# A decoder trunk on one core: the order of two weight rests, the key rests and the maxima in VectorE's stream of the attention heads

## The chip, the core and the metric

The kernel runs on one core of one Trainium2 chip. A core has TensorE for matrix products (the profile splits it into PE, the matmuls, and PEld, the loads of their stationary operand), VectorE (DVE), ScalarE (ACT), GpSimd (POOL) and SyncE (SP), which issues the transfers. Each engine works through its own list of instructions in order, and engines wait for one another by semaphores. The metric is the device time of one execution in microseconds, the median of three runs.

## The reference

Input `x` has 512 tokens of 1024 features in float32. Two layers, each:

```python
h = h + 0.5 * _swiglu(_rmsnorm(h, ffn1_norm[l]), ffn1_w1[l], ffn1_w3[l], ffn1_w2[l])
u = _rmsnorm(h, mix_norm[l])
z = u @ w_in[l]          # q, k, v of three attention branches, forget logits, gates
o_a = _diff_attention(...)         # 4 heads, difference of two softmaxes
o_b = _forgetting_attention(...)   # 8 heads, softmax with a forget bias
o_c = _stick_breaking_attention(...)   # 8 heads
m = sum of gates[:, :, i] * (o_i @ proj_i[l]);  h = h + m @ w_out[l]
h = h + 0.5 * _swiglu(_rmsnorm(h, ffn2_norm[l]), ...)
```

The branch that matters here is the second one:

```python
logits = (jnp.einsum('bqhd,bkhd->bhqk', qb, k).astype(f32) * scale
          + cq[..., :, None] - c[..., None, :])
logits = jnp.where(dist >= 0, logits, -jnp.inf)
p = jax.nn.softmax(logits, axis=-1)
return jnp.einsum('bhqk,bkhe->bhqe', p.astype(v.dtype), v)
```

## The kernel before

**Products in parts.** Every float32 operand of a product is split into a rounded part (`hi`, made by ScalarE) and a rest (`lo`, made by VectorE as operand minus rounded part), and `three` (L724) multiplies hi by hi, hi by lo and lo by hi. A *weight rest* is therefore one VectorE instruction over a whole unit of weights: `split(k)` (L2034) waits for ScalarE's rounded part and writes `w_lo` of slot `k`, 128 x 1024 elements. Its semaphore `w_set` lets TensorE use the slot and lets SyncE load the next unit into the raw slot (`load_next`, L600).

**The heads.** The attention runs over four tiles of 128 columns (two heads of the branches with 64-wide heads) in each of two layers, so the code in question runs 8 times: in the chain of waits its transposes start at 413.79, 484.89, 556.01 and 627.10 us (tiles 0 to 3 of the first layer) and at 1619.90, 1690.99, 1762.11 and 1833.22 us (the second layer). Within one tile every engine has its list written out by hand: `heads` of TensorE at L1105, of ScalarE at L1732, of VectorE at L2699. TensorE fills its time between attention steps with `unit(...)`: 8 blocks of three 512-column matmuls each, which project queries or keys for later steps.

**The piece around the change.** TensorE's list has this order (each step named by its line in the profile): `turn_probs(0)` (L1003, transposes of the third branch's weights), a unit up to block 6 (L726 to L728), `weighted(t, 2, 1)` (L1047), `scores(1, 0)` (L981, the second branch's first head), the rest of the unit, `unit(own[3], 2, 0, 4)` (12 matmuls with slot 2), `turn_probs(0)` again (L1003, ten transposes of the probabilities of `scores(1, 0)`), and the remaining blocks. Three waits matter:

- `scores(1, 0)` waits on `qk_set` for two steps of VectorE, the last of which is `qk_lo(1, 2, 1)`: the *rests of the second branch's keys*, two instructions of 64 x 512. That step in turn waits on `qk_hi_set` for ScalarE's `qk_hi(1, 2, 1)` (four ACTIVATEs of 64 x 512).
- `turn_probs` waits on `prob_set` once for each block `i` of 128 queries, ahead of the block's `i + 1` transposes (1, 2, 3 and 4). VectorE makes each block in two steps: `block_max` (L2576), a masked copy of the scores with their maximum, and `share_out` (L2582), a reciprocal (L2585) and a scaling (L2588), the *quotients*. Between them ScalarE takes the exponential, `exps` (L1655, in the profile L1659), one for each block.
- `unit(own[3], 2, ...)` waits on `w_set` for the rest of slot 2, and the next tile's `unit(0, 0)` for the rest of slot 0, `split(0)`.

`output_whole(1)` (L2666, in the profile L2669) adds the two parts of an attention output and waits for ScalarE's `output_rest(1)`. `turned_lo` (L2613, in the profile L2032 `area<-ps,area`) makes the rests of transposed probabilities. Nearly all rests show line L2032, so in the profile they are told apart by their tiles: `w_lo<-w_raw,w_hi` is a weight rest, `area<-scratch_whole,area` 64 x 512 a query or key rest.

Of the kernel before, what the change touches and what calls it, by code (L numbers as in the profile page):

```python
# [192 lines left out]
def trunk(nc, x, stream, params, const, const_r, const_b, out):  # L193
    ctx = ExitStack()
    with ctx:
# [57 lines left out]
        def half(hd):  # L253

            return slice(hd * HEAD, (hd + 1) * HEAD)
# [9 lines left out]
        def q_twice(branch, hd):  # L265
            return qk_tile(branch % 2 * 8 + hd)

        def k_both(branch, hd):
            return qk_tile(branch % 2 * 8 + 2 + hd)
# [3 lines left out]
        def q_rest(branch, hd):  # L273
            return qk_tile(16 + hd if branch == 2 else branch * 8 + 4 + hd)
# [26 lines left out]
        def tile(k):  # L301
            return scratch[:, k * SEQ:(k + 1) * SEQ]
# [963 lines left out]
        def neg_max(buf, i):  # L1266
            return stat[:, 4 * buf + i:4 * buf + i + 1]

        def total(buf, i):
            return stat[:, 8 + 4 * buf + i:9 + 4 * buf + i]  # L1270

        def inverse(buf, i):
            return stat[:, 16 + 4 * buf + i:17 + 4 * buf + i]
# [17 lines left out]
        def keys(part, j):  # L1291

            return area[:, part + PT_OFF[j]:part + PT_OFF[j] + (NQ - j) * P]

        def query_block(buf, i):
            return prob[buf][:, Q_OFF[i]:Q_OFF[i] + (i + 1) * P]
# [726 lines left out]
        def _(dve):  # L2023
# [7 lines left out]
            def lo(dst, src, hi_part):  # L2031
                return dve.tensor_tensor(dst, src, hi_part.bitcast(F32), ALU.subtract)  # L2032

            def split(k, raw=None, blocks=UNIT):  # L2034
                dve.wait_ge(w_hi_set, c.next(w_hi_set))
                at = slice(k * UNIT * P, (k * UNIT + blocks) * P)
                raw = k if raw is None else raw
                lo(w_lo[:, at], w_raw[:, raw * UNIT * P:(raw * UNIT + blocks) * P], w_hi[:, at]).then_inc(w_set, 1)
                c.skip(w_set)
# [520 lines left out]
            def qk_lo(branch, which, k):  # L2560
                dve.wait_ge(qk_hi_set, c.next(qk_hi_set))
                for hd in range(2):
                    src = tile(k)[half(hd), :]
                    if which == 0:
                        last = lo(q_rest(branch, hd)[half(hd), :], src, q_twice(branch, hd)[half(hd), :])
                    else:
                        last = lo(k_both(branch, hd)[half(1 - hd), :], src, k_both(branch, hd)[half(hd), :])
                last.then_inc(qk_set, 1)
                c.skip(qk_set)
# [6 lines left out]
            def block_max(buf, i):  # L2576
                dve.wait_ge(score_set, scored.next())
                dve.tensor_tensor_reduce(query_block(buf, i), ps[:, SB0 + i, 0:(i + 1) * P],  # L2578
                                         causal_w[:, (NQ - 1 - i) * P:], -1.0, FAR, ALU.add, ALU.min,
                                         neg_max(buf, i)).then_inc(max_set, 1)  # L2580

            def share_out(buf, i, done):  # L2582

                dve.wait_ge(exp_set, c.next(exp_set))
                dve.reciprocal(inverse(buf, i), total(buf, i)).then_inc(vec_done, 1)  # L2585
                dve.wait_ge(vec_done, c.next(vec_done))
                q = query_block(buf, i)
                dve.tensor_scalar(q, q, inverse(buf, i), None, ALU.mult).then_inc(done, 1)  # L2588
                c.skip(done)
# [23 lines left out]
            def turned_lo(j):  # L2613
                dve.wait_ge(pt_hi_set, c.next(pt_hi_set))
                lo(keys(PT_LO, j), ps[:, SB0 + j, 0:(NQ - j) * P], keys(PT_HI, j)).then_inc(pt_set, 1)
# [19 lines left out]
            def output_square_lo():  # L2635

                dve.wait_ge(o_sq_hi_set, c.next(o_sq_hi_set))
                lo(o_sq_lo, tile(7), o_sq_hi).then_inc(o_sq, 1)
# [37 lines left out]
            def rest_of_tile(t, layer, next_unit):  # L2676

                turned_lo(0)
                turned_lo(1)
                turned_lo(2)  # L2680
                turned_lo(3)
                next_unit(0, 0, SCALE)
                values_split() if t < NT else split(0)
                block_max(0, 0)
                block_max(0, 1)
                block_max(0, 2)
                block_max(0, 3)
                output_whole(1)
                share_out_all(0)
                block_max(1, 0)  # L2690
                block_max(1, 1)
                block_max(1, 2)
                block_max(1, 3)
                next_unit(1, 1, 1.0)
                split(1)
                output_lo(1, t - 1)
                differences(layer)

            def heads(t, layer, before):  # L2699

                if before:
                    rest_of_tile(t, layer, take)
                    qk_lo(2, 0, 0)
                    qk_lo(2, 2, 1)
                    turned_lo(0)
                    turned_lo(1)
                    turned_lo(2)
                    turned_lo(3)
                    values_lo(t, 0, before)
                    values_lo(t, 1, before)  # L2710
                    output_square_lo()
                c.skip(unit_done, 3)
                stick_runs(0)
                stick_runs(1)
                stick_weights(0)
                stick_runs(2)
                stick_weights(1)
                stick_runs(3)
                stick_weights(2)
                stick_weights(3)  # L2720
                if not before:
                    values_lo(t, 0, before)
                    values_lo(t, 1, before)
                    sums_of_forget(layer)
                split(2)
                if before:
                    output_normed(layer)
                    output_lo(0, t - 1)
                turned_lo(0)
                turned_lo(1)  # L2730
                turned_lo(2)
                turned_lo(3)
                values_lo(t, 2, before)
                values_lo(t, 3, before)
                split(0)
                split(1)
                output_whole(0)
                stick_runs(0)
                stick_runs(1)
                stick_weights(0)  # L2740
                stick_runs(2)
                stick_weights(1)
                stick_runs(3)
                stick_weights(2)
                stick_weights(3)
                banks = (AUX, 0, 1, AUX) if before else (0, AUX, 1, AUX)
                take(0, banks[0], SCALE)
                rows(t * 2, 1, 0)
                rows(t * 2 + 1, 1, 1)
                rows(t + N_FOX, 0, 0)  # L2750
                rows(t + N_FOX, 0, 1)
                take(1, banks[1], 1.0)
                qk_lo(1, 0, 0)
                turned_lo(0)
                turned_lo(1)
                turned_lo(2)
                turned_lo(3)
                split(2)
                qk_lo(1, 2, 1)
                split(0)  # L2760
                output_whole(1)
                block_max(0, 0)
                block_max(0, 1)
                block_max(0, 2)
                block_max(0, 3)
                share_out(0, 0, prob_set)
                share_out(0, 1, prob_set)
                share_out(0, 2, prob_set)
                share_out(0, 3, prob_set)
                take(0, banks[2], SCALE)  # L2770
                split(1)
                turned_lo(0)
                turned_lo(1)
                turned_lo(2)
                turned_lo(3)
                take(1, banks[3], 1.0)
                block_max(1, 0)
                block_max(1, 1)
                block_max(1, 2)
                block_max(1, 3)  # L2780
                qk_lo(0, 0, 0)
                share_out(1, 0, prob_set)
                output_lo(2, t)
                share_out(1, 1, prob_set)
                share_out(1, 2, prob_set)
                share_out(1, 3, prob_set)
                output_whole(0)
                qk_lo(0, 2, 1)
                split(2)
# [152 lines left out]
            def mixer(layer, gain):  # L2942
                forget(layer)
                heads(0, layer, False)
                for t in range(1, NT):
                    heads(t, layer, True)
# [254 lines left out]
```

## Time and profile before

| what | value |
|---|---|
| median of 3 runs | 2435.03 us (2434.97 to 2435.12) |
| profiled execution | 2435.02 us |
| its span, first to last instruction | 2433.0 us |
| PE busy / PEld busy | 2421.7 us (100%) / 2226.9 us (92%) |
| DVE busy / ACT busy | 2125.6 us (87%) / 1498.7 us (62%) |
| granted TensorE clock | 1.000 over the span |
| one tile of the heads, from 484.89 to 556.01 | 71.12 us |

The profiled execution lasted 2.02 us more than its span, and it lies 0.01 us from the median. PE's busy time counts pipelined matmuls whose ends are modelled, so a busy share of 100% does not say that no matmul waited: a wait shows in the distance between the starts of two neighbours, and in the idle time ahead of a weight load.

### The profile page before, as it was taken

To read this page: it belongs to the slowest core of one execution; us is meant where nothing else is said; L and a number is where in the kernel's file an instruction comes from. 1 tells how busy PE (TensorE), PEld (TensorE's weight loads), DVE (VectorE), ACT (ScalarE), POOL (GpSimd) and SP (SyncE) were. 2 spreads that over 40 slices of the span, in tenths; PEclk is the share of its full clock that TensorE was granted. 3 is DMA by queue.
4 is the path that set the end of the run, shared out by engine and by line. 5 is a ranking of instruction groups with operands and counts; after the bars stand their busy time and mean duration, and the time that the engine had idled before them with its cause. 6 is when DMAs were issued, how large, how long until landed. Compare 5 with 4: busy or idle time off the path is not lost.

```text
span 2433.0 us, 48313 instructions
## 1 busy us (share of the span) xinstructions
PE 2421.7 (100%) x15618; PEld 2226.9 (92%) x15618; DVE 2125.6 (87%) x3968; ACT 1498.7 (62%) x2951; POOL 3.2 (0%) x10
## 2 busy tenths in 40 slices
PE   9999999999999999999999999999999999999999
PEld 8999888888899889998889998888888998899988
DVE  8999878989898779998799997799988986899986
ACT  6666457788754456664366664578786554566643
POOL 0000000000000000000000000000000000000000
PEclk9999999999999999999999999999999999999999
DMA  4333322222232323333333323322212333233332
GB/s 166 110 103 104 113 96 69 70 62 69 71 113 80 112 87 105 104 106 117 109 94 109 103 95 105 111 72 61 70 61 70 104 109 101 87 109 104 115 113 78
DMA packets 64676, 233.72 MB, mean 96 GB/s; under 512 B 7168, under 2 KB 7552, under 8 KB 64512
## 3 DMA queue, kind: packets, MB, share of 16 engines
q1 hardware_dynamic: 64368, 231.58, 29.4%
q8 instruction: 85, 1.39, 0.2%
q14 instruction: 79, 0.65, 0.1%
q10 hardware_dynamic: 144, 0.10, 0.0%
HBM read 229.55 MB, written 2.10 MB: 95 GB/s over the span
## 4 chain that ended last, share of the span: by engine, by line
PE 87%; DVE 6%; ACT 4%; issue 3%; DMA 0%; DVEq 0%; ACTq 0%; SPq 0%
PE ps L726 26%; PE ps L728 26%; PE ps L727 26%; DVE area L2032 2%; PE ps L1047 2%; PE ps L981 1%; ACT area L1311 1%; PE ps L1029 1%; PE ps L1031 1%; PE ps L1030 1%; ACT scratch_whole L1659 1%; PE ps L1003 1%; DVE w_lo L2032 1%; DVE scratch_whole L2578 1%; DVE scratch_whole L2598 0%
## 5 line engine op out<-in xcount | busy, mean ns | idle before, releaser
L1311 ACT ACTIVATE w_hi<-w_raw 128x512 fp32r<-128x512 f32 (+2 forms) x882 | 623.0, 717 | 481.4 <-PE ps L728 218.7
L2032 DVE TENSOR_TENSOR w_lo<-w_raw,w_hi 128x512 fp32r<-128x512 f32 (+2 forms) x882 | 699.2, 800 | 102.2 <-ACT w_hi L1311 84.8
L726 PE MATMUL ps<-u_hi,w_hi 128*128 128x256 f32 (+1 forms) x2240 | 708.5, 316 | 0.0
L728 PE MATMUL ps<-u_hi,w_lo 128*128 128x256 f32 (+1 forms) x2240 | 706.0, 315 | 0.0
L727 PE MATMUL ps<-u_lo,w_hi 128*128 128x256 f32 (+1 forms) x2240 | 705.6, 315 | 0.0
L727 PE MATMUL ps<-area,w_hi 128*128 128x256 f32 (+1 forms) x1778 | 583.3, 328 | 0.0
L726 PE MATMUL ps<-area,w_hi 128*128 128x512 f32 (+1 forms) x1414 | 482.3, 341 | 1.0 <-ACT scratch_whole L1417 0.9
L728 PE MATMUL ps<-area,w_lo 128*128 128x512 f32 (+1 forms) x1414 | 480.1, 340 | 0.0
L728 PEld LDWEIGHTS ps<-u_hi,w_lo 128*128 128x128 f32 x2240 | 427.1, 191 | 27.2
L726 PEld LDWEIGHTS ps<-u_hi,w_hi 128*128 128x128 f32 x2240 | 427.2, 191 | 26.7 <-DVE w_lo L2032 0.5
L727 PEld LDWEIGHTS ps<-u_lo,w_hi 128*128 128x128 f32 x2240 | 427.3, 191 | 25.9
L727 PEld LDWEIGHTS ps<-area,w_hi 128*128 128x128 f32 x1778 | 338.1, 190 | 29.2
L726 PEld LDWEIGHTS ps<-area,w_hi 128*128 128x128 f32 x1414 | 268.1, 190 | 32.5 <-DVE w_lo L2032 1.6
L728 PEld LDWEIGHTS ps<-area,w_lo 128*128 128x128 f32 x1414 | 268.1, 190 | 29.5
L726 PE MATMUL ps<-v_area,w_hi 128*128 128x256 f32 x880 | 249.4, 283 | 0.0
L728 PE MATMUL ps<-v_area,w_lo 128*128 128x256 f32 x880 | 249.0, 283 | 0.0
L1417 ACT ACTIVATE scratch_whole<-ps 128x256 f32<-128x256 f32 x376 | 141.7, 378 | 151.9 <-PE ps L728 150.2
L726 PEld LDWEIGHTS ps<-v_area,w_hi 128*128 128x128 f32 x880 | 168.9, 192 | 0.4 <-DVE w_lo L2032 0.2
L728 PEld LDWEIGHTS ps<-v_area,w_lo 128*128 128x128 f32 x880 | 168.9, 192 | 0.0
L1311 ACT ACTIVATE area<-scratch_whole 64x512 fp32r<-64x512 f32 (+1 forms) x202 | 123.6, 627 | 38.7 <-DVE scratch_whole L2558 14.2
L727 PE MATMUL ps<-v_area,w_hi 128*128 128x256 f32 x440 | 124.5, 283 | 0.0
L2032 DVE TENSOR_TENSOR area<-scratch_whole,area 64x512 fp32r<-64x512 f32 (+1 forms) x120 | 82.3, 686 | 12.5 <-ACT area L1311 11.2
(214 smaller groups left out, 3172.6 us busy)
## 6 DMA issues: line engine op xcount, KB each, us to landing
w_raw<-weights SPq DMA_DIRECT2D x432, 512.0 KB, 3.7
h<-x SPq DMA_DIRECT2D x4, 512.0 KB, 6.5
out<-scratch_whole SPq DMA_DIRECT2D x8, 256.0 KB, 2.4
scratch_whole<-const_b SPq DMA_DIRECT2D x1, 512.0 KB, 9.5
scratch_whole<-const_r SPq DMA_DIRECT2D x1, 192.0 KB, 8.7
cst<-const SPq DMA_DIRECT2D x1, 137.0 KB, 8.1
par<-params ACTq DMA_DIRECT2D x1, 98.0 KB, 4.5
```

Of the source, the lines that this page charges most:

```text
L726: pe.matmul(dst, hi, x_hi, start=start, stop=False, **kw)
L727: pe.matmul(dst, hi, x_lo, start=False, stop=False, **kw)
L728: return pe.matmul(dst, lo, x_hi, start=False, stop=stop, **kw)
L981: last = pe.matmul(ps[:, SB0 + i, 0:n], queries[part][:, i * P:n], keys_of[part][:, 0:n], start=part == 0, stop=part == 1)
L1003: last = pe.transpose(ps[:, SB0 + j, (i - j) * P:(i - j + 1) * P], prob[buf][:, at:at + P], ident)
L1029: pe.matmul(dst, x_hi, w_hi[:, of], start=k == 0, stop=False)
L1030: pe.matmul(dst, x_lo, w_hi[:, of], start=False, stop=False)
L1031: last = pe.matmul(dst, x_hi, w_lo[:, of], start=False, stop=k == UNIT - 1)
L1047: last = pe.matmul(ps[:, OB, SEQ - n:SEQ], v, area[:, at + PT_OFF[j]:at + PT_OFF[j] + n], start=(j, part) == (0, 0), stop=(j, part) == ste ...
L1311: return act.activation(dst, src, ACT.Copy)
L1417: act.activation(to, half_bank((of or banks(s))[2 if n == 1 else 0]), ACT.Copy).then_inc(snap_set, 1)
L2032: return dve.tensor_tensor(dst, src, hi_part.bitcast(F32), ALU.subtract)
```

## The change

In VectorE's list of `heads` the rests of the second branch's keys, `qk_lo(1, 2, 1)`, stand ahead of the rest of slot 2 and no longer behind it. The rest of slot 0 stands behind the four maxima and ahead of the four quotients, and no longer ahead of `output_whole(1)` and the maxima. No instruction is added or removed, and the lists of the other engines are the same.

```diff
--- before.py
+++ after.py
@@ -2755,14 +2755,14 @@
                 turned_lo(1)
                 turned_lo(2)
                 turned_lo(3)
+                qk_lo(1, 2, 1)
                 split(2)
-                qk_lo(1, 2, 1)
-                split(0)
                 output_whole(1)
                 block_max(0, 0)
                 block_max(0, 1)
                 block_max(0, 2)
                 block_max(0, 3)
+                split(0)
                 share_out(0, 0, prob_set)
                 share_out(0, 1, prob_set)
                 share_out(0, 2, prob_set)
```

The first place is VectorE's list in tile 1 of the first layer, from the last instruction of `turned_lo` on; `64x512 x2` is the pair of key rests, `w_lo` is slot 2 first and slot 0 second. Before:

```order
L2032 TENSOR_TENSOR area<-ps,area 128x128
L2035 REGISTER_ALU
L2032 TENSOR_TENSOR w_lo<-w_raw,w_hi 128x1024
L2561 REGISTER_ALU
L2032 TENSOR_TENSOR area<-scratch_whole,area 64x512 x2
L2035 REGISTER_ALU
L2032 TENSOR_TENSOR w_lo<-w_raw,w_hi 128x1024
L2668 REGISTER_ALU
L2669 TENSOR_TENSOR w_raw<-ps,w_raw 64x512
L2578 ISA scratch_whole,stat<-ps,masks 128x128
```

Now:

```order
L2032 TENSOR_TENSOR area<-ps,area 128x128
L2561 REGISTER_ALU
L2032 TENSOR_TENSOR area<-scratch_whole,area 64x512 x2
L2035 REGISTER_ALU
L2032 TENSOR_TENSOR w_lo<-w_raw,w_hi 128x1024
L2668 REGISTER_ALU
L2669 TENSOR_TENSOR w_raw<-ps,w_raw 64x512
L2578 ISA scratch_whole,stat<-ps,masks 128x128
```

The key rests have moved up past the first weight rest, and the second weight rest is gone from ahead of L2669.

The second place is a few instructions further on, from the last of the four maxima (L2578, of the block of 512 keys) to the first two quotients. Before:

```order
L2578 ISA scratch_whole,stat<-ps,masks 128x512
L2578 ISA stat 128x1
L2584 REGISTER_ALU
L2585 RECIPROCAL stat<-stat 128x1
L2586 REGISTER_ALU
L2588 TENSOR_SCALAR scratch_whole<-scratch_whole,stat 128x128
L2584 REGISTER_ALU
L2585 RECIPROCAL stat<-stat 128x1
L2586 REGISTER_ALU
L2588 TENSOR_SCALAR scratch_whole<-scratch_whole,stat 128x256
```

Now:

```order
L2578 ISA scratch_whole,stat<-ps,masks 128x512
L2578 ISA stat 128x1
L2035 REGISTER_ALU
L2032 TENSOR_TENSOR w_lo<-w_raw,w_hi 128x1024
L2584 REGISTER_ALU
L2585 RECIPROCAL stat<-stat 128x1
L2586 REGISTER_ALU
L2588 TENSOR_SCALAR scratch_whole<-scratch_whole,stat 128x128
L2584 REGISTER_ALU
L2585 RECIPROCAL stat<-stat 128x1
L2586 REGISTER_ALU
L2588 TENSOR_SCALAR scratch_whole<-scratch_whole,stat 128x256
```

The rest of slot 0 stands between the last maximum and the first reciprocal. The same two places differ in all 8 tiles.

## Rows read from the trace of the kernel before

**Rows 1.** Busy time by engine of one stretch: PE, PEld, DVE, ACT, POOL, PEclk, DMA

```profile
469.31:484.89 15.58, 15.58 (x80) 13.16 (x79) 14.77 (x35) 12.41 (x25) 0.00 (x0) 1.00 0.21 68
```

**Rows 2.** Timeline of VectorE, tile 1: start us, us, line, what [idle before <- releaser]

```profile
476.55 1.21 DVE L2032 TENSOR_TENSOR w_lo<-w_raw,w_hi 128x1024 fp32r<-128x1024 f32 x1
477.79 1.39 DVE L2032 TENSOR_TENSOR area<-scratch_whole,area 64x512 fp32r<-64x512 f32 x2
479.21 1.22 DVE L2032 TENSOR_TENSOR w_lo<-w_raw,w_hi 128x1024 fp32r<-128x1024 f32 x1
480.47 0.69 DVE L2669 TENSOR_TENSOR w_raw<-ps,w_raw 64x512 f32<-64x512 f32 x1
...
482.23 0.69 DVE L2578 CUSTOM_DVE_ANT_0 scratch_whole<-ps,masks 128x512 f32<-128x512 f32 x1
...
482.84 0.16 DVE L2585 RECIPROCAL stat<-stat 128x1 f32<-128x1 f32 x1
...
484.42 0.49 DVE L2588 TENSOR_SCALAR scratch_whole<-scratch_whole,stat 128x512 f32<-128x512 f32 x1
...
486.65 1.68 DVE L2032 TENSOR_TENSOR area<-ps,area 128x512 fp32r<-128x512 f32 x4
488.76 0.69 DVE L2558 SCALAR_TENSOR_TENSOR scratch_whole<-ps,rstd 128x512 f32<-128x512 f32 x1 [0.42 <-PE ps L728]
490.31 0.29 DVE L2578 CUSTOM_DVE_ANT_0 scratch_whole<-ps,masks 128x128 f32<-128x128 f32 x1 [0.86 <-PE ps L981]
```

**Rows 3.** Timeline of ScalarE, the same tile

```profile
475.36 2.31 ACT L1311 ACTIVATE area<-scratch_whole 64x512 fp32r<-64x512 f32 x4
...
483.82 0.19 ACT L1659 ACTIVATION_READ_ACCUMULATOR scratch_whole<-scratch_whole,stat 128x1 f32 x1
...
499.13 1.17 ACT L1311 ACTIVATE w_hi<-w_raw 128x128 fp32r<-128x128 f32 x2
```

**Rows 4.** Timeline of TensorE's matmuls, the same tile

```profile
479.23 1.54 PE L981 MATMUL ps<-area 128*128 128x128 f32 x8
...
484.49 0.40 PE L728 MATMUL ps<-u_hi,w_lo 128*128 128x512 f32 x1
484.73 1.26 PE L1003 MATMUL ps<-cst,scratch_whole 128*128 128x128 f32 x10
485.74 0.48 PE L726 MATMUL ps<-u_hi,w_hi 128*128 128x512 f32 x1
```

**Rows 5.** Timeline of TensorE's weight loads between 485.38 and 485.50

```profile
485.28 0.36 PEld L1003 LDWEIGHTS ps<-cst,scratch_whole 128*128 128x128 f32 x3
```

**Rows 6.** Timelines of four engines, tile 0

```profile
404.34 2.31 ACT L1311 ACTIVATE area<-scratch_whole 64x512 fp32r<-64x512 f32 x4
...
406.69 1.39 DVE L2032 TENSOR_TENSOR area<-scratch_whole,area 64x512 fp32r<-64x512 f32 x2 [0.18 <-ACT area L1311]
...
413.31 0.49 DVE L2588 TENSOR_SCALAR scratch_whole<-scratch_whole,stat 128x512 f32<-128x512 f32 x1
...
413.39 1.25 PEld L1003 LDWEIGHTS ps<-cst,scratch_whole 128*128 128x128 f32 x10
...
414.63 0.48 PE L726 MATMUL ps<-u_hi,w_hi 128*128 128x512 f32 x1
```

**Rows 7.** Timelines, other transposes behind VectorE (the last tile's differences)

```profile
653.55 1.94 DVE L2610 SCALAR_TENSOR_TENSOR scratch_whole<-scratch_whole,stat 128x128 f32<-128x128 f32 x4
...
655.54 0.42 PEld L1003 LDWEIGHTS ps<-cst,scratch_whole 128*128 128x128 f32 x4 [0.35 <-DVE scratch_whole L2610]
...
654.38 1.81 PE L1003 MATMUL ps<-cst,scratch_whole 128*128 128x128 f32 x10
...
655.95 0.47 PE L726 MATMUL ps<-u_hi,w_hi 128*128 128x512 f32 x1
```

**Rows 8.** Waits of weight loads: waiter <- releaser: us, times, longest

```profile
PEld ps L1047 <- DVE area L2032: 7.7, 22, 0.5
```

**Rows 9.** The page, DMA issues: count, KB each, median us to landing

```profile
w_raw<-weights SPq DMA_DIRECT2D x432, 512.0 KB, 3.7
```

## The prediction, made before the changed kernel was run

> **What bounds the kernel now.** I read the busy times first. In the table of the profile PE is busy for the whole span and VectorE for 87% of it. In the 15.6 us ahead of the transposes in question PE is busy for all of it and VectorE for 14.77 us, at a granted clock of 1.00; the same stretch of the other seven tiles agrees within 0.4 us for PE and 0.1 us for VectorE [rows 1]. So TensorE sets the time, VectorE has next to no room beside it, and every moment for which VectorE makes TensorE wait is added to the end. Then I read the waits. TensorE hardly waits here: all rests of that kind hold its weight loads back for 7.7 us in 22 places over the span [rows 8]. What matters is therefore not what the removed waits cost, but which new one appears. For that I read the timelines of VectorE, ScalarE and TensorE side by side in tile 1, and ask at each step who is waited for.
>
> **Part one, the key rests ahead of the weight rest of slot 2.** Before, this weight rest runs from 476.55 to 477.76 and the key rests from 477.79 to 479.18 [rows 2]. They need ScalarE's rounded keys, and these end at 475.36 + 2.31 = 477.67 [rows 3]. So moved up, the key rests can't start with the weight rest's 476.55; VectorE waits until 477.67 and starts at about 477.70 (in tile 0 the same step starts 0.04 us after ScalarE's end: 404.34 + 2.31 = 406.65 against 406.69 [rows 6]). The gain is 477.79 - 477.70 = 0.09 us, and 1.1 us in which VectorE did a weight rest become idle. TensorE starts the scores at 479.23 [rows 4], 0.05 us behind the end of the key rests; it may start them up to 0.09 us earlier. In tile 0 the step already waits for ScalarE, so nothing is gained there. The rest of slot 2 now runs from about 479.1 to 480.35. Its user, the unit ahead of the transposes, has 12 matmuls; L1003 starts at 484.73, 0.24 us behind the last of them [rows 4], and 12 such distances put the unit's start near 481.9. It is covered by 1.5 us, so I cost it at nothing. Without that cover it would cost 1.2 us a tile.
>
> **Part two, the rest of slot 0 ahead of the quotients.** `output_whole` starts at 480.47 before. Now it follows the rest of slot 2, which holds the place that the rest of slot 0 had; it starts 0.09 us earlier, and so do the maxima. Before, the first reciprocal starts at 482.84, right behind the last maximum, whose main part started at 482.23 and lasted 0.69 us [rows 2]. Now a weight rest stands there. How much it puts between its own start and the next start the rows bound: 1.26 us (479.21 to 480.47) and 1.24 us (476.55 to 477.79) on the one side [rows 2]; on the other, its duration of 1.22 us less the 0.08 us by which the reciprocal starts before the maximum's end (482.92 - 482.84), so 1.14 us. I take 1.20. The quotients thus shift by 1.20 - 0.09 = 1.11 us in the six later tiles and by 1.20 in tile 0 of each layer.
>
> Does something hide that? ScalarE's last exponential ends at 483.82 + 0.19 = 484.01 [rows 3], and the first ones long before 482.84: before the change the quotients wait for VectorE's own queue, not for ScalarE, so the weight rest fills no gap there.
>
> What is late next are the transposes. The last quotient ends at 484.42 + 0.49 = 484.91 [rows 2], and the first of the four weight loads that need it starts at 485.28 [rows 5] (the seventh of ten). The margin is 0.37 us, against a shift of 1.11. The new end of the last quotient is 484.91 + 1.11 = 486.02. What TensorE does with a late block the trace shows elsewhere: the differences end at 653.55 + 1.94 = 655.49, the seventh weight load starts at 655.54, and the next unit's matmul at 655.95 [rows 7]: 0.05 us, then 0.41 us. By these the load starts at 486.07 and the unit at 486.48, against 485.74 before [rows 4]: 0.74 us. In tile 0 the last quotient ends at 413.31 + 0.49 = 413.80, now 415.00; the unit starts at 415.46 against 414.63 [rows 6]: 0.83 us.
>
> **Whether it passes on.** The next step of VectorE that takes its time from TensorE comes soon: it has idle times of 0.42 us (until 488.76, for a unit) and 0.86 us (until 490.31, for the scores of the other head) [rows 2]. VectorE reaches them 1.11 us later, TensorE 0.74 us later; the 0.37 us between are less than the first idle time. From 490.31 on the two stand to each other as before, all 0.74 us later. The probability rests between (486.65 before [rows 2], now near 487.8) are needed by a weighted product that starts at about 489.3 now, 12 matmuls of 0.24 us behind 486.48: covered. The raw slot 0 is released near 484.0 and not at 480.43; the next unit takes 3.7 us to land [rows 9] and ScalarE reads it at 499.13 [rows 3]: covered by over 11 us.
>
> Sum: 6 x 0.74 + 2 x 0.83 = 6.1 us, with 1.14 and 1.26 for the open distance 5.6 and 6.6. On the profiled execution's own 2435.02 us that is 2441.1 us; the median of the runs, 2435.03, is the same for this purpose.
>
> **A rule weighed.** In the stretch of [rows 1] the weight loads are busy for 13.16 of 15.58 us. The Trainium skill, Perfetto Trace Analysis, section Identifying the Most-Contended Engine, says that matmul busy time is no measure of TensorE's headroom and the weight loads' busy share is. By that rule TensorE would have 16% in hand here, and a stall of 0.74 us would be made up within 5 us: no change. The trace doesn't show such a recovery: behind the late transposes of [rows 7] the ten take 655.95 - 654.38 = 1.57 us against 485.74 - 484.73 = 1.01 us undisturbed [rows 4]: 0.56 us longer, of which the 0.35 us that the seventh weight load waited is a part, and nothing came faster than in the undisturbed case.
>
> **The rivals.**
> 1. *The stall is made up* (2435.0 to 2437.3 us, within 0.2%). For it: TensorE waits later in a tile anyway, 7.7 us over the 22 places [rows 8], 0.96 us a tile. If those waits ended at fixed times the new stall would take their place and all of it would vanish (2435.0); if half of them did, 6.1 - 8 x 0.48 = 2.3 us are left (2437.3). Against it: the rests that end them hang on maxima that start when TensorE's scores arrive (idle 0.86 us for L981 [rows 2]), so they shift as well.
> 2. *The quotients keep up, and only the earlier keys count* (2434.5 us, not slower). Place: the last quotient of each tile. If the weight rest came out of VectorE's way, the last quotient would end before 485.23 in tile 1 (0.05 us ahead of the load at 485.28), and the scores up to 0.09 us earlier in six tiles would be all: -0.5 us. It decides where the shift is below 0.32 us. For it stands only that VectorE overlaps neighbours by some hundredths; against it 1.22 us of work against a margin of 0.37.
> 3. *A second stall behind the first* (2444.7 us). The probability rests start 1.11 us later and the weighted product then waits: if the product needed all four rests at its start, 487.8 + 1.68 = 489.45 against 489.3, and the same happened again at the next head, 0.45 us a tile would come on top: 6.1 + 3.6 = 9.7 us. Against it: the product takes the rests one after another, and the last of them only behind several matmuls.
>
> **How the numbers follow.** What a measurement of this kernel can tell from no change is about 0.2%, 4.9 us. The forecast has 76%, rival 1 has 11%, rival 2 has 4%, rival 3 has 5%, and 4% is left for a smaller stall. The forecast's own range is 2440.6 to 2441.7, all of it slower by over 0.2% (from 2439.9 on), though it would take only 0.15 us less in each tile to fall under that bound; I leave 4% of the forecast's case for it. Rival 2 lies within 0.2% too, and no case that I can name is faster by more; 2% stand for one that I can't. So slower 0.77, same 0.21, faster 0.02. The range for 8 times in 10 is 2438.0 to 2442.5.
>
> **What would show it.** In the changed profile VectorE should be idle for about 1.1 us ahead of the key rests, for ScalarE. L1003's weight loads should wait for L2588 in all 8 tiles, 6 to 7 us in all (no such row exists before), its ten transposes should take about 1.75 us from start to the next unit, and the tile should last 71.8 to 71.9 us. It is wrong if the ten take 1.01 us as before; if they take longer but the tile lasts 71.1 us, rival 1 holds; if the weighted product (L1047) behind them gains a wait, rival 3.

## The result and the profile after

The changed kernel takes 2441.01 us (median of 12 runs, 2440.52 to 2441.26) against 2435.27 us of the kernel before beside it (12 runs, 2434.97 to 2435.82): 1.0023 times as long, 95% interval 1.0015 to 1.0031. 2441.1 us were forecast: 6.1 us more than the 2435.03 of before, where 5.74 us were measured (2441.01 - 2435.27). The profiled execution took 2440.52 us with a span of 2438.6 us, 5.6 us more than the span before, at a granted clock of 1.00.

VectorE in tile 1 of the changed kernel (start us, us, line, what, idle before and its releaser), to be laid beside [rows 2]:

```profile
478.48 1.39 DVE L2032 TENSOR_TENSOR area<-scratch_whole,area 64x512 fp32r<-64x512 f32 x2 [1.06 <-ACT area L1311]
479.90 1.23 DVE L2032 TENSOR_TENSOR w_lo<-w_raw,w_hi 128x1024 fp32r<-128x1024 f32 x1
481.15 0.69 DVE L2669 TENSOR_TENSOR w_raw<-ps,w_raw 64x512 f32<-64x512 f32 x1
...
482.92 0.69 DVE L2578 CUSTOM_DVE_ANT_0 scratch_whole<-ps,masks 128x512 f32<-128x512 f32 x1
...
483.53 1.22 DVE L2032 TENSOR_TENSOR w_lo<-w_raw,w_hi 128x1024 fp32r<-128x1024 f32 x1
484.67 0.16 DVE L2585 RECIPROCAL stat<-stat 128x1 f32<-128x1 f32 x1
...
486.24 0.49 DVE L2588 TENSOR_SCALAR scratch_whole<-scratch_whole,stat 128x512 f32<-128x512 f32 x1
...
488.37 1.68 DVE L2032 TENSOR_TENSOR area<-ps,area 128x512 fp32r<-128x512 f32 x4
490.23 0.69 DVE L2558 SCALAR_TENSOR_TENSOR scratch_whole<-ps,rstd 128x512 f32<-128x512 f32 x1 [0.18 <-PE ps L728]
491.78 0.29 DVE L2578 CUSTOM_DVE_ANT_0 scratch_whole<-ps,masks 128x128 f32<-128x128 f32 x1 [0.85 <-PE ps L981]
```

All of this tile lies 0.77 us later than before, by what tile 0 lost, so only distances within the tile can be compared. ScalarE's keys end here:

```profile
476.14 2.31 ACT L1311 ACTIVATE area<-scratch_whole 64x512 fp32r<-64x512 f32 x4
```

at 476.14 + 2.31 = 478.45, and VectorE, idle for 1.06 us, starts the key rests at 478.48. From the end of ScalarE's keys to the last maximum it is 482.92 - 478.45 = 4.47 us; before it was 482.23 - 477.67 = 4.56 [rows 2, 3]. So the move up gained the 0.09 us that ScalarE left to gain. From the last maximum to the last quotient it is 486.24 - 482.92 = 3.32 us against 484.42 - 482.23 = 2.19: 1.13 us more, which is the weight rest that stands there now.

TensorE's weight loads for the transposes at the same place:

```profile
485.20 0.14 PEld L1003 LDWEIGHTS ps<-cst,scratch_whole 128*128 128x128 f32 x1
485.66 0.20 PEld L1003 LDWEIGHTS ps<-cst,scratch_whole 128*128 128x128 f32 x2 [0.32 <-DVE scratch_whole L2588]
486.19 0.31 PEld L1003 LDWEIGHTS ps<-cst,scratch_whole 128*128 128x128 f32 x3 [0.33 <-DVE scratch_whole L2588]
486.78 0.42 PEld L1003 LDWEIGHTS ps<-cst,scratch_whole 128*128 128x128 f32 x4 [0.28 <-DVE scratch_whole L2588]
```

and its matmuls, the ten transposes and the first of the unit behind:

```profile
485.42 2.02 PE L1003 MATMUL ps<-cst,scratch_whole 128*128 128x128 f32 x10
487.19 0.48 PE L726 MATMUL ps<-u_hi,w_hi 128*128 128x512 f32 x1
```

Before, the ten loads were one row without idle time (in tile 0 they are shown in [rows 6]). Now each block of quotients behind the first is waited for, and the unit behind starts 487.19 - 485.42 = 1.77 us after the first transpose, not 1.01 [rows 4]. In tile 0 the unit starts at 415.40 instead of 414.63: 0.77 us. In tile 1 the transposes take 0.76 us longer, but TensorE reaches them 0.08 us earlier in the tile, since the scores ahead of them can start earlier; from tile 0's unit to tile 1's it is 487.19 - 415.40 = 71.79 us, against 485.74 - 414.63 = 71.11 before, a loss of 0.68 us. Over the span the waits of weight loads (us, times, longest) read

```profile
PEld ps L1047 <- DVE area L2032: 7.8, 22, 0.5
PEld ps L1003 <- DVE scratch_whole L2588: 7.4, 24, 0.3
```

L2588 is new, 24 times, which is three blocks in each of eight tiles; L1047 is what it was [rows 8]. The three waits of a tile add up to 0.93 us and the transposes take only 0.76 us longer. A part of such a wait costs nothing, because the loads run ahead of their matmuls: the first by 485.42 - 485.20 = 0.22 us.

### The profile page after: what moved, and what is told of

Same layout as the page of the kernel before. It is cut to its first block, busy times and chain, and to the rows that moved or that the text cites. A ratio compares the mean times of both kernels' runs of the same rounds, so it can differ in the third digit from the quotient of the medians.

```text
span 2438.6 us, 48313 instructions
## 1 busy us (share of the span) xinstructions
PE 2425.6 (99%) x15618; PEld 2225.2 (91%) x15618; DVE 2125.1 (87%) x3968; ACT 1498.4 (61%) x2951; POOL 3.2 (0%) x10
## 4 chain that ended last, share of the span: by engine, by line
PE 82%; DVE 9%; ACT 5%; issue 4%; DVEq 0%; DMA 0%; ACTq 0%; SPq 0%
PE ps L726 25%; PE ps L727 25%; PE ps L728 25%; ACT area L1311 3%; DVE area L2032 2%; DVE w_lo L2032 2%; PE ps L1047 1%; PE ps L1029 1%; PE ps L1031 1%; PE ps L1030 1%; ACT scratch_whole L1659 1%; DVE scratch_whole L2578 1%; PE ps L1003 1%; DVE scratch_whole L2623 1%; PE ps L981 1%
## 5 line engine op out<-in xcount | busy, mean ns | idle before, releaser
L726 PE MATMUL ps<-u_hi,w_hi 128*128 128x256 f32 (+1 forms) x2240 | 708.8, 316 | 0.5 <-DVE w_lo L2032 0.5
L726 PE MATMUL ps<-area,w_hi 128*128 128x512 f32 (+1 forms) x1414 | 482.3, 341 | 1.0 <-ACT scratch_whole L1417 0.9
L726 PEld LDWEIGHTS ps<-u_hi,w_hi 128*128 128x128 f32 x2240 | 427.2, 191 | 27.7 <-DVE w_lo L2032 1.7
L726 PEld LDWEIGHTS ps<-area,w_hi 128*128 128x128 f32 x1414 | 268.1, 190 | 32.8 <-DVE w_lo L2032 1.6
L726 PE MATMUL ps<-v_area,w_hi 128*128 128x256 f32 x880 | 249.4, 283 | 0.0
L1417 ACT ACTIVATE scratch_whole<-ps 128x256 f32<-128x256 f32 x376 | 141.5, 377 | 151.8 <-PE ps L728 150.1
L726 PEld LDWEIGHTS ps<-v_area,w_hi 128*128 128x128 f32 x880 | 168.9, 192 | 0.4 <-DVE w_lo L2032 0.2
```

The lines of the kernel that those rows point to most:

```text
L726: pe.matmul(dst, hi, x_hi, start=start, stop=False, **kw)
L1417: act.activation(to, half_bank((of or banks(s))[2 if n == 1 else 0]), ACT.Copy).then_inc(snap_set, 1)
```

## The experiments

The first question was which of the two moves costs, and whether a late quotient is paid in full. Each group of kernels ran on one chip together with the kernel before, and each time is compared with the time of the kernel before on that chip.

**Only the key rests moved.**

```diff
-                split(2)
                 qk_lo(1, 2, 1)
+                split(2)
                 split(0)
                 output_whole(1)
```

> Only the key rests are moved ahead of the rest of slot 2; the rest of slot 0 stays ahead of output_whole and the maxima. Theory (the key rests wait 1.1 us for ScalarE and everything behind them is late, wherever the second weight rest stands): output_whole starts 1.15 to 1.25 us later than before, the last quotient too, and the ten transposes of the branch's first head stall as in the changed kernel: +5.3 to +6 us, about 2441 us. Rival (what costs is the weight rest between the maxima and the quotients, and the earlier keys cost nothing): 2434.7 to 2435.4 us, no wait of L1003 for L2588.

Measured: 2440.88 us against 2435.24, ratio 1.0023 (1.0014 to 1.0032): all of the loss, with the rest of slot 0 still ahead of `output_whole`. VectorE's rows:

```profile
478.36 1.39 DVE L2032 TENSOR_TENSOR area<-scratch_whole,area 64x512 fp32r<-64x512 f32 x2 [1.06 <-ACT area L1311]
479.78 2.36 DVE L2032 TENSOR_TENSOR w_lo<-w_raw,w_hi 128x1024 fp32r<-128x1024 f32 x2
482.17 0.69 DVE L2669 TENSOR_TENSOR w_raw<-ps,w_raw 64x512 f32<-64x512 f32 x1
...
486.12 0.49 DVE L2588 TENSOR_SCALAR scratch_whole<-scratch_whole,stat 128x512 f32<-128x512 f32 x1
```

VectorE's idle 1.06 us reach `output_whole`: it starts 482.17 - 478.36 = 3.81 us behind the start of the key rests, where before it started 480.47 - 477.79 = 2.68 us behind it [rows 2], because now both weight rests stand between. That is 1.13 us more (1.15 to 1.25 were expected), while the key rests themselves gain at most 0.09. L1003 waits for L2588 for 7.4 us in 24 places, as in the changed kernel. The rival, by which the earlier keys cost nothing and only a weight rest ahead of the quotients costs, falls: the first move alone is enough.

**Only the rest of slot 0 moved.**

```diff
                 split(2)
                 qk_lo(1, 2, 1)
-                split(0)
                 output_whole(1)
                 block_max(0, 0)
                 block_max(0, 1)
                 block_max(0, 2)
                 block_max(0, 3)
+                split(0)
```

> Only the rest of slot 0 is moved behind the maxima; the key rests stay behind the rest of slot 2. Theory: output_whole, freed of 1.25 us of queue, can only start 0.5 us earlier in the later tiles because ScalarE's part ends at 479.94 in the trace before (0.9 us earlier in tile 0), then the weight rest adds 1.14 to 1.2: the last quotient is 0.65 to 0.7 us late in six tiles and 0.25 to 0.3 in two, against a margin of 0.37. So 6 x 0.3 = 1.8 to 2 us more, about 2437.2 us. Rival (the move costs the whole weight rest, 1.2 - 0.37 a tile, whatever stands in front): 2441.5 us.

Measured: 2436.88 us (2436.68 to 2437.39) against 2435.24 (2435.02 to 2435.74); the ratio's interval, 0.9998 to 1.0016, includes 1, but the two sets of runs don't overlap. VectorE's rows:

```profile
480.15 0.69 DVE L2669 TENSOR_TENSOR w_raw<-ps,w_raw 64x512 f32<-64x512 f32 x1 [0.80 <-ACT w_raw L1699]
...
485.23 0.49 DVE L2588 TENSOR_SCALAR scratch_whole<-scratch_whole,stat 128x512 f32<-128x512 f32 x1
```

and the last four weight loads of the transposes:

```profile
485.77 0.42 PEld L1003 LDWEIGHTS ps<-cst,scratch_whole 128*128 128x128 f32 x4 [0.28 <-DVE scratch_whole L2588]
```

Without the weight rest in front, VectorE comes to `output_whole` early and waits there for ScalarE, 0.80 us (0.35 us in tile 0). So of the 1.25 us that the move frees ahead of `output_whole` only a part is used, and the whole weight rest comes back ahead of the quotients. The last quotient is late by the difference, and only the last block is waited for: loads of L1003 wait 1.7 us for L2588 in 6 places, none of them in tile 0. That makes 1.6 us where 1.8 to 2 were expected; the rival's 2441.5 us falls.

**The rest of slot 0 behind the quotients**, with the key rests moved and without.

```diff
+                qk_lo(1, 2, 1)
                 split(2)
-                qk_lo(1, 2, 1)
-                split(0)
                 output_whole(1)
...
                 share_out(0, 3, prob_set)
+                split(0)
```

> The key rests are moved up as in the changed kernel, and the rest of slot 0 stands behind the quotients instead of ahead of them. Theory (the quotients alone carry the loss): no wait of L1003 for L2588; the probability rests behind come about 1.1 us later than before and just miss the weighted product by 0.1 to 0.15 us a tile, the scores start 0.08 us earlier: 2435.0 to 2436.2 us. Rival (VectorE is so full that the same 1.1 us of idling costs the same wherever it surfaces): 2440 to 2441 us, with new waits of L1047.

> The key rests stay behind the rest of slot 2, the rest of slot 0 stands behind the quotients. Theory: the quotients end 0.5 us earlier than before, which nobody uses, and the probability rests start about 0.75 us later, in time for the weighted product: within 0.5 us of before, 2435.3 us. Rival (as above, lost VectorE time costs wherever it surfaces): 0.75 - 0.37 us a tile or more, 2438 us.

Measured: 2434.95 us (2434.71 to 2435.3) with the key rests moved, 2435.35 (2435.03 to 2435.86) without (where `split(2)` and `qk_lo` keep their order), against 2435.24: ratios 0.9999 (0.9990 to 1.0008) and 1.0001 (0.9992 to 1.0010), which can't be told from no difference. In the first, VectorE idles as in the changed kernel, and the quotients are not late:

```profile
477.65 1.39 DVE L2032 TENSOR_TENSOR area<-scratch_whole,area 64x512 fp32r<-64x512 f32 x2 [1.06 <-ACT area L1311]
...
484.27 0.49 DVE L2588 TENSOR_SCALAR scratch_whole<-scratch_whole,stat 128x512 f32<-128x512 f32 x1
...
487.54 1.68 DVE L2032 TENSOR_TENSOR area<-ps,area 128x512 fp32r<-128x512 f32 x4
...
490.21 0.29 DVE L2578 CUSTOM_DVE_ANT_0 scratch_whole<-ps,masks 128x128 f32<-128x128 f32 x1 [0.39 <-PE ps L981]
```

and TensorE's transposes and unit:

```profile
484.58 1.26 PE L1003 MATMUL ps<-cst,scratch_whole 128*128 128x128 f32 x10
485.59 0.48 PE L726 MATMUL ps<-u_hi,w_hi 128*128 128x512 f32 x1
```

The unit starts 1.01 us behind the transposes again, and no load of L1003 waits for L2588. The probability rests start later, at 487.54 against 486.65 [rows 2]. The idle time ahead of VectorE's next steps takes that up: the 0.42 us of before are gone and the 0.86 us are down to 0.39. L1047's waits are what they were (7.6 us in 22 places). So the rival by which lost time of VectorE costs the same wherever it surfaces falls: it costs ahead of the quotients, and nothing between them and the other head's scores.

**Doses of VectorE time.** The kernel before, with a part or all of the rest of slot 0 computed once or twice more, which only adds VectorE time ahead of the maxima:

```diff
                 qk_lo(1, 2, 1)
+                dve.wait_ge(w_hi_set, c.peek(w_hi_set))
+                for _ in range(1):     # 2 in the third
+                    lo(w_lo[:, 0:1024], w_raw[:, 0:1024], w_hi[:, 0:1024]).then_inc(vec_done, 1)   # 0:256 in the first
+                    dve.wait_ge(vec_done, c.next(vec_done))
                 split(0)
```

> The kernel before, with 256 columns of the rest of slot 0 computed once more ahead of it (with a semaphore wait behind, so the result is the same): about 0.45 us more in VectorE's queue ahead of the maxima in each of 8 tiles. Theory (a late quotient costs shift minus 0.37 us a tile, and nothing is made up): 8 x 0.1 = 0.8 us, 2436.1 us, with waits of L1003 for L2588 of well under 0.2 us each. Rival (TensorE makes short stalls up within the tile): no change, 2435.3 us.

> The same with all 1024 columns computed once more: about 1.27 us more in VectorE's queue in each tile, with the order of before. Theory: (1.27 - 0.37) x 8 = 7.2 us, 2442.5 us, tile 71.12 + 0.9 = 72.0 us. Rival (stalls are made up): at most 2437.3 us.

> The same with 1024 columns computed twice more: about 2.55 us more in each tile. Theory: (2.55 - 0.37) x 8 = 17.4 us, 2452.7 us, so one more rest costs its full 1.27 us a tile once the margin is used up. Rival (stalls are made up, up to the 0.96 us a tile in which TensorE waits elsewhere): 9.5 to 10 us, 2445 us.

> The changed kernel again on the same chip as the three doses, for comparison: 2441.0 us, 5.7 us over before. A shift of the last quotient of 1.1 us with the theory's rule gives 0.69 to 0.77 us a tile.

| kernel | median us | range us (runs) | over 2434.99 of before | expected |
|---|---|---|---|---|
| 256 columns | 2436.07 | 2435.86 to 2436.17 (11) | 1.08 | 0.8 |
| 1024 columns | 2442.62 | 2442.37 to 2443.01 (6) | 7.63 | 7.2 |
| 2 x 1024 columns | 2454.44 | 2452.69 to 2458.79 (5) | 19.45 | 17.4 |
| the changed kernel | 2440.67 | 2440.34 to 2441.06 (11) | 5.68 | 5.7 |

Ratios and intervals: 1.0004 (0.9995 to 1.0013), 1.0031 (1.0019 to 1.0044), 1.0084 (1.0070 to 1.0098), 1.0023 (1.0014 to 1.0032). The interval of the first includes 1, but its fastest run (2435.86) is above the slowest of before (2435.39). The first two follow "shift less 0.37 us in each tile". In the kernel with 256 columns `output_whole` starts 481.10 - 479.38 = 1.72 us behind the first of the two weight rests, where it started 1.26 us behind the one of before, a shift of 0.46 us (VectorE's timeline in tile 1):

```profile
479.38 1.69 DVE L2032 TENSOR_TENSOR w_lo<-w_raw,w_hi 128x256 fp32r<-128x256 f32 x2
481.10 0.69 DVE L2669 TENSOR_TENSOR w_raw<-ps,w_raw 64x512 f32<-64x512 f32 x1
```

and TensorE's unit starts 1.11 us behind the first transpose instead of 1.01:

```profile
484.90 1.36 PE L1003 MATMUL ps<-cst,scratch_whole 128*128 128x128 f32 x10
486.01 0.47 PE L726 MATMUL ps<-u_hi,w_hi 128*128 128x512 f32 x1
```

In the kernel with 1024 columns `output_whole` starts 2.51 us behind the doubled rest's start instead of 1.26, a shift of 1.25 (VectorE's timeline):

```profile
479.98 2.48 DVE L2032 TENSOR_TENSOR w_lo<-w_raw,w_hi 128x1024 fp32r<-128x1024 f32 x2
482.49 0.69 DVE L2669 TENSOR_TENSOR w_raw<-ps,w_raw 64x512 f32<-64x512 f32 x1
```

and TensorE's unit starts 1.91 us behind the first transpose instead of 1.01:

```profile
485.49 2.15 PE L1003 MATMUL ps<-cst,scratch_whole 128*128 128x128 f32 x10
487.40 0.48 PE L726 MATMUL ps<-u_hi,w_hi 128*128 128x512 f32 x1
```

Nothing is made up later: the whole 8 x 0.9 = 7.2 us are in the time. Both times lie 0.3 to 0.4 us above the rule. In both traces 0.32 us of that is a wait outside the heads that the trace before doesn't have, of L726 for ScalarE's L1417 (at 928.43 and 931.52 us). The third kernel lies above its expectation by 2 us, and its runs spread over 6 us. Its profile shows 1.6 us of that in tile 0: busy times of PE, PEld, DVE, ACT and POOL in four stretches, with the granted clock, the DMA share and GB/s behind them:

```profile
415.00:416.00 1.00, 0.78 (x6) 0.48 (x5) 0.93 (x5) 1.00 (x3) 0.00 (x0) 1.00 0.02 8
...
417.00:418.00 1.00, 1.00 (x4) 0.73 (x3) 1.00 (x2) 1.00 (x3) 0.00 (x0) 0.50 0.00 0
418.00:419.00 1.00, 1.00 (x4) 0.81 (x3) 1.00 (x3) 0.98 (x3) 0.00 (x0) 0.50 0.02 8
...
421.00:425.00 4.00, 4.00 (x24) 3.57 (x23) 2.79 (x10) 2.38 (x9) 0.00 (x0) 1.00 0.02 9
```

TensorE's timeline there:

```profile
414.73 2.24 PE L1003 MATMUL ps<-cst,scratch_whole 128*128 128x128 f32 x10 [1.01 <-DVE scratch_whole L2588]
...
417.51 0.63 PE L728 MATMUL ps<-u_hi,w_lo 128*128 128x512 f32 x1
417.94 0.63 PE L726 MATMUL ps<-u_hi,w_hi 128*128 128x512 f32 x1
```

Behind the long wait the granted clock is 0.50, that is 1.2 instead of 2.4 GHz, between about 417 and 420 us, and matmuls of 512 columns follow at 0.43 us. The eight or so started there cost 8 x (0.43 - 0.23) = 1.6 us. In tile 1 of the same execution the first load waits 1.44 us and the clock stays at 1.00, so what decides is open. The two fastest runs, 2452.69 and 2452.86 us, lie 17.7 and 17.9 us above before, close to the rule's 17.4; their granted clock over the span is 1.000, against 0.999 in the profiled execution and 0.998 and 0.997 in the two slowest (2457.8 and 2458.79). So more stretches at the low clock are the likely cause of the slowest two, which no trace shows.

**A rule taken too far.** By then the reading was that order costs where a step that TensorE reaches soon stands behind one that it reaches late. Two waits of L1047 in the kernel before looked like such places: at 499.96 behind the last rest of slot 2, and at 517.09 behind the third branch's key rests. TensorE's weight loads before:

```profile
499.96 0.30 PEld L1047 LDWEIGHTS ps<-area 128*128 128x128 f32 x2 [0.51 <-DVE area L2032]
...
517.09 2.00 PEld L1047 LDWEIGHTS ps<-area 128*128 128x128 f32 x12 [0.38 <-DVE area L2032]
```

The first kernel moves the last rest of slot 2:

```diff
                 qk_lo(0, 2, 1)          # end of heads
-                split(2)
...
                 turned_lo(3)            # rest_of_tile
+                split(2)
                 next_unit(0, 0, SCALE)
```

> The order of before, except that the last rest of slot 2 in heads stands behind the four probability rests of the next rest_of_tile, whose weighted product TensorE reaches first (before: a weight load of L1047 at 499.96 waits 0.51 us and one at 500.42 waits 0.17 us for VectorE, matmul starts 0.24 and 0.18 us late). Theory (the order on VectorE costs where a step that TensorE reaches soon stands behind one that it reaches late): both waits go in all 8 tiles, 8 x 0.4 = 3.2 us less: 2431.9 us. Rival (the probability rests are bound by ScalarE or by the transposes, not by the queue): 2434.8 to 2435.3 us.

Measured: 2438.44 us (2438.09 to 2438.79) against 2435.2, ratio 1.0013 (1.0004 to 1.0022): slower by 3.2 us, where a gain of as much was expected. This expectation missed, for the same reason for which the changed kernel loses. VectorE's timeline:

```profile
499.19 1.69 DVE L2032 TENSOR_TENSOR area<-ps,area 128x512 fp32r<-128x512 f32 x4 [0.42 <-ACT area L1311]
...
517.45 1.69 DVE L2032 TENSOR_TENSOR area<-ps,area 128x512 fp32r<-128x512 f32 x4
```

TensorE's weighted product:

```profile
518.20 2.06 PE L1047 MATMUL ps<-area 128*128 128x512 f32 x11 [0.90 <-DVE area L2032]
```

and the waits of its weight loads over the span:

```profile
PEld ps L1047 <- DVE area L2032: 7.3, 6, 1.2
PEld ps L1003 <- DVE scratch_whole L2610: 3.2, 8, 0.7
```

The early waits are gone (6 of 22 places are left), and TensorE is 0.4 us earlier up to the transposes ahead of 517. But the weight rest had covered VectorE's wait for ScalarE's rounding of the first transposed block; with it moved, VectorE idles 0.42 us at 499.19. From there to 517 it idles only as before (0.2 us twice), so it is late there. TensorE's matmuls wait 0.90 us at 518.20, where before they started some 0.23 us late. That takes back the early gain and 0.34 us more: from the transposes at 485.44 to those of the next tile it is 71.46 us, against 71.12. The rest of the loss goes with the waits of L1003 for the first branch's differences (L2610), 3.2 us in 8 places instead of 1.2 in 4; how much of it they cost is open.

> In addition, the rests of the third branch's keys (qk_lo(2, 2, 1)) stand behind the probability rests and the two value rests in tiles 1 to 3, so that the weighted product at 517.09 in the trace before need not wait for them (0.23 us late there). Theory: 6 x 0.2 = 1.2 to 1.4 us less again: 2430.6 us. Rival (the keys or values then come late for the scores at 520.7 or for the value products): no change against slot2_late or slower, with a new wait of L981 or L1029.

The second of these kernels has in addition, in `heads`:

```diff
                     qk_lo(2, 0, 0)
-                    qk_lo(2, 2, 1)
                     turned_lo(0)
...
                     values_lo(t, 1, before)
+                    qk_lo(2, 2, 1)
```

It takes 2434.05 us (2433.77 to 2434.46) against 2435.2, ratio 0.9995 (0.9986 to 1.0004): 4.4 us less than the first, since it takes away the wait that had grown (waits of L1047 are down to 2.0 us in 6 places). The forecast of 2430.6 fell with that of the kernel that it builds on. The sign of its rival is there as well, though small: the third branch's keys now come late for the scores, and L981's waits, 1.0 us in 2 places before, read

```profile
PEld ps L981 <- DVE area L2032: 2.7, 8, 0.5
```

> The same, with the part of the changed kernel that loses nothing: second branch's key rests ahead of the rest of slot 2, and the rest of slot 0 behind the quotients. Theory: 0.3 to 0.5 us less again, 2430.2 us. Rival: the gains overlap or the added idle time of VectorE (1.1 us a tile) surfaces now: 2430.6 us or more.

Measured: 2433.92 us (2433.67 to 2434.56), ratio 0.9995 (0.9986 to 1.0004); 0.13 us less than the kernel above, which can't be told from nothing. The 0.3 to 0.5 us less that were expected didn't come.

> The key rests ahead of the rest of slot 2 and the rest of slot 0 behind the quotients (keys_rest_behind), and the third branch's key rests behind the probability and value rests (the second move of slot2_keys_late), but the last rest of slot 2 where it was before, where it covers a wait for ScalarE. Theory: 0.3 us from the first pair of moves and 6 x 0.23 = 1.4 us from the 0.23 us of L1047 at 517.09: 2433.5 us, faster than all_three (2433.9). Rival (slot 2's move gained its 0.4 us a tile after all and lost it only to the keys): slower than all_three by 1 us or more, 2435 us.

Measured: 2432.74 us (2432.56 to 2432.93) against 2434.83 (2434.62 to 2435.09) of before, ratio 0.9991 (0.9982 to 1.0000): 2.1 us less than the kernel before, where 1.7 us less were expected, and the fastest of all. Its waits of weight loads:

```profile
PEld ps L1047 <- DVE area L2032: 5.3, 16, 0.5
```

and TensorE's transposes and weighted product in the place where 517.09 was, before

```profile
513.66 1.25 PE L1003 MATMUL ps<-cst,scratch_whole 128*128 128x128 f32 x10
```

and now

```profile
513.21 1.25 PE L1003 MATMUL ps<-cst,scratch_whole 128*128 128x128 f32 x10
...
516.41 2.03 PE L1047 MATMUL ps<-area 128*128 128x512 f32 x12
```

From the transposes to the weighted product it is 516.41 - 513.21 = 3.20 us, against 517.09 - 513.66 = 3.43 in the trace before, six times; and the waits of L1047 fell from 7.7 us in 22 places to 5.3 in 16. The interval just reaches 1.0000, but the slowest run of this kernel is 1.7 us below the fastest of before. The rival, by which the moved rest of slot 2 had been worth its 0.4 us a tile, falls: against its own time of before this kernel gains 2.1 us and the one with slot 2's rest moved 1.3. The traces differ where that rest was blamed: L1003 waits for L2610 for 1.2 us in 4 places here, as before, and for 3.2 in 8 there; L981 waits 1.0 us in 2 places here and 2.6 in 8 there.

## Why the prediction was right

- *The time.* The mechanism came as forecast, but that 2441.1 and 2441.01 agree to 0.1 us is in part luck. The forecast difference of 6.1 us was 0.4 us too large, and the kernel before took 2435.27 us in these runs and not the 2435.03 that the forecast was added to.
- *The key rests can't go up by more than 0.09 us.* Shown: 4.47 against 4.56 us, and the first move alone costs the whole 5.6 us. The prediction kept two things apart: idle time of VectorE in part one, which it charged with nothing, and a weight rest inserted ahead of the quotients in part two, which it charged with everything. They are one loss: the same instructions stand ahead of the last quotient before and after the change, and what is added is the idle 1.06 us. Whether the rest of slot 0 stands ahead of `output_whole` or ahead of the quotients makes no difference then (2440.88 and 2441.01 us).
- *Distance that the weight rest adds, 1.14 to 1.26, taken as 1.20.* It was 484.67 - 483.53 = 1.14, the lower end. This is the term that was sized too large: with 1.14 the rule gives 6 x 0.68 + 2 x 0.77 = 5.6 us, which is the difference of the spans, and 0.68 and 0.77 us are what tiles 1 and 0 lost.
- *The margin of the last quotient, 0.37 us.* Shown by two doses: 0.46 us of shift cost 0.10 us a tile, 1.25 us cost 0.90.
- *Only the last block was reckoned.* In fact three blocks are waited for (0.32, 0.33, 0.28 us), 7.4 us in all where 6 to 7 were forecast. The end is the same, since the last quotient sets when the last four transposes can start, and the earlier waits lie within that time. The other signs came as forecast: VectorE idle for 1.06 us (1.1), 1.77 us from the first transpose to the unit (1.75), and 71.79 us from tile to tile (71.8 to 71.9).
- *Rival 1, the stall is made up,* falls by the doses: a stall of 0.9 us a tile arrives at the end in full. The Trainium skill, Perfetto Trace Analysis, section Identifying the Most-Contended Engine, judges TensorE's headroom by MFU (its arithmetic as a share of the peak) and by the weight loads' busy share. The second is 84% in the stretch of [rows 1]. The prediction weighed what would follow if the other 16% were time in hand, and the doses show that they are not: in this kernel the gaps between the weight loads make up no stall.
- *Rival 2*, by which the quotients keep up, fell with the 24 new waits. *Rival 3*, a second stall, fell with L1047's waits unchanged.
- *What passes on:* VectorE's idle 0.42 and 0.86 us became 0.18 and 0.85 in the changed kernel. So the first took up by how much VectorE was later than TensorE, as forecast, though only 0.24 us of it where 0.37 were reckoned; the steps ahead of it are closer together (486.24 to 488.37 against 484.42 to 486.65, 0.10 us less).

## What to carry to other kernels

An instruction that stands in front of one that waits for another engine may be covering that wait: before moving it, look up when the awaited engine is done, for the instruction behind can start no earlier than that, whenever the queue gets there. When VectorE has no idle time up to the next thing that TensorE needs, lost VectorE time is paid in full, less the margin there (0.37 us here). In this kernel the same weight rest cost nothing once it stood behind that point, with idle time of VectorE behind it to take up the delay; so look for such a place. A wait that disappears from the list is no gain until the next one down the same queue has been read as well.

## What was not expected of the hardware

A single wait of TensorE of about 1.4 us (its matmuls idle for 1.01 us), with short waits around it, was followed by some 3 us at a granted clock of 0.50 in one of the tiles of the largest dose; in the other seven tiles of that execution the same waits left it at 1.00, and so did the 0.90 us of the matmuls in the kernel with slot 2's rest moved, in the six tiles that have them. The same largest dose has runs from 2452.69 to 2458.79 us, where the runs of each other kernel lie within 0.9 us.
